# Products of zeros on TensorE in the last four experts of each expert layer

## The reference

```python
def hierarchical_moe(x, w_rg, w_re, w_gate, w_up, w_down):
    """x: (B,S,D). Top-1 expert group, then top-2 SwiGLU experts within it."""
    ...
    for g in range(N_GROUPS):
        hid = jax.nn.silu(jnp.einsum('nd,edf->nef', xt, w_gate[g])) * \
            jnp.einsum('nd,edf->nef', xt, w_up[g])
        hid = hid * combine[:, g, :, None].astype(hid.dtype)
        out = out + jnp.einsum('nef,efd->nd', hid, w_down[g],
                               preferred_element_type=jnp.float32)
    return out.astype(x.dtype).reshape(b, s, d)
```

## Time and profile before

| | us |
|---|---|
| median of 3 runs | 603.98 |
| all runs | 609.18, 601.09, 603.98 |
| the profiled execution | 608.75 |
| its span on the core | 607.0 |
| TensorE (PE) busy | 546.9 (90%) |
| weight loads of TensorE (PEld) busy | 301.7 (50%) |
| VectorE (DVE) busy | 178.7 (29%) |
| ScalarE (ACT) busy | 172.3 (28%) |
| HBM read and written | 388 GB/s over the span |

### The profile page before, as it was taken

The page is one execution under the profiler, slowest core; times in us unless marked ns, Lnnn a source line. Parts: engine busy times, 40 slices in busy tenths (PEclk is TensorE's granted clock), DMA queues, the critical chain, the costliest instruction groups (busy, mean ns, idle before and its releaser), DMA issues.

```text
span 607.0 us, 7989 instructions
## 1 busy us (share of the span) xinstructions
PE 546.9 (90%) x3338; PEld 301.7 (50%) x3338; DVE 178.7 (29%) x306; ACT 172.3 (28%) x307; POOL 6.5 (1%) x16
## 2 busy tenths in 40 slices
PE   5999899999999998668799999999999999987766
PEld 4888687444424441312288878774444344423111
DVE  3686944311101110100374465353111011101001
ACT  4845734111111110000384777341111111100100
POOL 0000000000000000000000000000000000000000
PEclk7999999999999998988799999999999999997877
DMA  8999999899999999999999955598999999999992
GB/s 307 423 420 418 422 419 421 313 425 419 421 421 419 421 421 422 421 419 419 421 419 419 422 211 205 220 423 319 425 421 420 418 421 422 421 419 421 417 419 109
DMA packets 33565, 236.14 MB, mean 389 GB/s; under 512 B 3760, under 2 KB 3760, under 8 KB 5488
## 3 DMA queue, kind: packets, MB, share of 16 engines
q1 hardware_dynamic: 32800, 232.07, 93.0%
q0 software_dynamic: 720, 3.45, 1.4%
HBM read 234.45 MB, written 1.05 MB: 388 GB/s over the span
## 4 chain that ended last, share of the span: by engine, by line
PE 65%; DMA 28%; DVE 3%; ACT 1%; issue 1%; SPq 1%; DVEq 0%; ACTq 0%
PE psum L1263 18%; DMA raw<-stream 18%; DMA late<-stream 9%; PE psum L262 8%; PE psum L263 8%; PE psum L264 8%; PE psum L1240 7%; PE psum L1311 7%; DMA xT<-x_turned 1%; PE psum L519 1%; PE psum L1325 1%; PE psum L336 1%; ACT hid L1384 1%; PE psum L1090 1%; SPq L209 1%
## 5 line engine op out<-in xcount | busy, mean ns | idle before, releaser
L1263 PE MATMUL psum<-raw,x 128*32 128x512 f32 x680 | 91.7, 641 | 22.0 <-DMA raw<-stream 11.8
L254 DVE TENSOR_TENSOR raw_lo<-raw,whi 128x1024 fp32r<-128x1024 f32 x52 | 62.5, 1222 | 47.9 <-ACT whi L247 47.7
L1311 PE MATMUL psum<-y,pickT 128*128 128x512 f32 x128 | 69.5, 668 | 4.5 <-ACT y L1390 3.5
L1240 PEld LDWEIGHTS psum<-pick,h 128*128 128x128 f32 x512 | 59.4, 193 | 18.4 <-issue 15.9
L247 ACT CAST whi<-raw 128x1024 fp32r<-128x1024 f32 x52 | 53.5, 1048 | 48.2 <-PE psum L264 41.3
L1240 PE MATMUL psum<-pick,h 128*128 128x128 f32 x512 | 63.6, 281 | 1.2 <-DVE pick L1207 1.0
L262 PE MATMUL psum<-whi,hnT_hi 128*128 128x512 f32 x144 | 58.1, 403 | 5.4 <-DVE hnT_lo L366 5.2
L1215 DVE TENSOR_TENSOR pick<-pick,lists 128x256 f32<-128x256 f32 x16 | 6.8, 424 | 178.1 <-PE psum L1325 178.1
L263 PE MATMUL psum<-whi,hnT_lo 128*128 128x512 f32 x144 | 57.8, 401 | 0.0
L264 PE MATMUL psum<-raw_lo,hnT_hi 128*128 128x512 f32 x144 | 57.4, 398 | 0.0
L1263 PE MATMUL psum<-raw,hid 128*32 128x512 f32 x376 | 48.8, 619 | 5.9 <-ACT hid L1384 5.1
(11 more groups left out here) (203 smaller groups left out, 493.3 us busy)
## 6 DMA issues: line engine op xcount, KB each, us to landing
raw<-stream SPq DMA_DIRECT2D x157, 1024.0 KB, 26.5
late<-stream SPq DMA_DIRECT2D x60, 1024.0 KB, 24.2
raw<-stream SPq DMA_DIRECT2D x2, 512.0 KB, 7.5
xT<-x_turned SPq DMA_DIRECT2D x2, 512.0 KB, 8.4
h<-x SPq DMA_DIRECT2D x1, 1024.0 KB, 12.3
pb<-even_bias POOLq DMA_DIRECT2D x1, 1024.0 KB, 13.9
pool_c<-even_pool POOLq DMA_DIRECT2D x1, 1024.0 KB, 9.4
pb<-even_bias POOLq DMA_DIRECT2D x1, 512.0 KB, 8.3
```

What stands on the lines that cost most here:

```text
L254: nc.vector.tensor_tensor(raw_lo[PLACE[c][0]][:, cols], chunk(c)[:, cols], whi[:, n % SPLIT, cols].bitcast(F32), ALU.subtract).then_inc(lo ...
L1240: mm = nc.tensor.matmul(psum[:, gather_banks(q)[part], kk * P:(kk + 1) * P], h[:, t, k * P:(k + 1) * P], pick[:, t, :], start=(t == 0), st ...
L1263: nc.tensor.matmul(psum[rows, b, :], lhs[:, rows], chunk(c)[:, e * W4:(e + 1) * W4], start=start, stop=stop).then_inc(moe_used, 1)
L1311: nc.tensor.matmul(bank(b), pickT[:, t * P:(t + 1) * P], y[:], start=(q == 0), stop=(q == QUADS - 1)).then_inc(m.scattered, 1)
```

## The change

`keep_warm_pe` gets a second argument, the PSUM bank that the product writes (3 if none is given). In quad 7 of each layer products of zeros are put between what TensorE does there: three behind each of the chunks k = 1 to 6 (behind the scatter, row scale or turn that follows the chunk, where there is one), five behind the last gate/up chunk, two behind the turn of `hid`, three behind down chunk 1, and three before the last scatter, these into bank 0. In layer 0 five more follow the last scatter. That makes 36 products in layer 0 and 31 in layer 1. No wait and no instruction of another engine changes. From line 280 on the line numbers shift by one, further down by up to twelve.

```diff
--- before.py
+++ after.py
@@ -276,9 +276,10 @@
 
         zeros_ready = sem("zeros_ready")
 
-        def keep_warm_pe(n):
+        def keep_warm_pe(n, b=3):
+
             for _ in range(n):
-                nc.tensor.matmul(bank(3), zeros[:], zeros[:].unsqueeze(1).to_broadcast([P, 4, P]), start=True, stop=True, skip_group_check=True)
+                nc.tensor.matmul(bank(b), zeros[:], zeros[:].unsqueeze(1).to_broadcast([P, 4, P]), start=True, stop=True, skip_group_check=True)
 
 
 
@@ -1341,18 +1342,29 @@
                         row_scale_pe(pe, layer, q)
                     if k == 4 and q:
                         turn_pick_pe(pe, layer, q)
+                    if q == QUADS - 1 and 1 <= k < GU_CHUNKS - 1:
+                        keep_warm_pe(3)
                 if q == 0:
                     turn_pick_pe(pe, layer, q)
                 if q < QUADS - 1:
                     gather_pe(pe, layer, q + 1, (0, 1))
+                if q == QUADS - 1:
+                    keep_warm_pe(5)
                 turn_hid_pe(pe, layer, q)
+                if q == QUADS - 1:
+                    keep_warm_pe(2)
                 for i in range(DOWN_CHUNKS):
                     down_pe(pe, layer, q, i)
+                    if q == QUADS - 1 and i == 1:
+                        keep_warm_pe(3)
                     if i == (1 if q == QUADS - 1 else 2):
                         scatter_pe(pe, layer, q, 0)
                     if q == QUADS - 1 and i == 2 and layer == 0:
                         turn_pe(pe, m.h_added, (2, 4), (0, 1))
+            keep_warm_pe(3, 0)
             scatter_pe(pe, layer, QUADS - 1, 1)
+            if layer == 0:
+                keep_warm_pe(5, 0)
 
         def pickT_act(act, layer, q):
             act.wait_ge(m.pickT_turned, no(layer, q) + 1)
```

## The result

| | before | after |
|---|---|---|
| median, us | 604.16 (6 runs) | 612.18 (6 runs) |
| lowest to highest | 601.09 to 609.18 | 610.88 to 615.25 |
| profiled execution, span | 607.0 | 609.5 |
| TensorE busy | 546.9 | 555.8 |

The ratio is 1.0119, with a 95% interval of 1.0081 to 1.0158. The changed kernel is slower by over 1%, where 601.7 was forecast; 612.18 lies even past the 611.2 that the prediction had as the bound of dear products.

The account below looks back on a forecast made before the run. DMA was taken to bound most of the kernel, TensorE 304 to 499 us and the tail. Layer 0 +1.1 and layer 1 -3.4 sum to -2.3, taken off the median 603.98: 601.7, own range 600 to 603, wide range 597.6 to 606.5.

Parts of the forecast that it names:

- the bound of dear products: Upper bound with 0.42 us for each product, 50 of them on the path: +7.2, giving 611.2 us.
- the step that costs the change in layer 1 by its products alone: Layer 1's last quad: sixth chunk from 581.2, products delay chunks, faster tail ends with last scatter at 598.5, not 601.90: -3.4.
- the sum: Step-by-step addition over both layers' last quads at 0.23 us per further product: +1.1 - 3.4 = -2.3 us.
- Rival C: Larger gain: new code length removes layer 0's 0.85 gap and raises the clock earlier, 599.2; or cheaper products, 597.6; chance 0.15.
- 216 ns product: Alternative price from the skill's figure: 67 products take 14.5 us instead of 15.4, the part on the path 0.5 less.
- Layer 0: Layer 0's last quad: groups delay the eighth chunk by 4.6, the faster tail wins part back; +1.1 us, all reaching the end.
- The step from one execution to the median: Profiled 608.75 becomes 606.45; the same difference taken off the median of three runs, 603.98, gives 601.7.
- Rival A: Layer 0, gate/up chunks 2 to 7: backlog wins, a little slower; at 0.31 per product 605.7; chance 0.25 together with D.
- Rival B: Tails stay at 1.2 GHz and products only cost: layer 0 +3.7, layer 1 +1.2, so 608.9; chance 0.07.
- D: No change at all: what layer 1 gains, layer 0 loses; 604; chance 0.25 together with Rival A.
- the split by 2%: Chances for the whole kernel: faster by over 2% 0.03, no change 0.94, slower 0.03.

Follow-up runs that it names:

- e7: Changed kernel plus 8 products in layer 1's skipped spill code, moving layer 1's restart by 16 instructions; 606.28 us, ratio to the kernel before 1.0031.
- e2: Changed kernel with the products of layer 1 alone; 603.74 us, ratio to the kernel before 1.0004.
- e4: Changed kernel plus 24 products in layer 0's skipped spill code, moving both layers' restarts by 48 instructions; 604.2 us, ratio to the kernel before 1.0003.
- e0: The kernel before once more, without any edit, for a second trace; 604.27 us, ratio 1.001.
- e8: Changed kernel with products in layer 1 alone, without groups behind chunks 1 to 4, plus 24 skipped products in either layer; 604.96 us, ratio to before 1.0.
- e6: Kernel before plus 24 products in the skipped spill code of either layer, so both restarts move; 606.1 us, ratio 1.0022.
- e9: Changed kernel without groups behind chunks 1 to 4 in both layers, plus 24 skipped products in layer 0; 601.23 us, ratio to before 0.9924.
- e1: Kernel before plus 36 products in layer 1's skipped spill code, putting its restart where the changed kernel has it; 604.75 us, ratio 1.001.
- e10: e9 plus 116 skipped products in layer 1, its restart 256 instructions behind its place in the changed kernel; 605.26 us, ratio to before 1.0027.
- e3: Changed kernel with the products of layer 0 alone; 605.99 us, ratio to the kernel before 1.0024.

## Why the prediction was wrong

- **What failed** is the step that costs the change in layer 1 by its products alone, from the old timeline, in which the two chunks behind the restart have no gap (it set out from 581.2). The products of layer 0 also moved layer 1's code, by 72 instructions, and the sum had no term for that. It measured 5.9 (e7 against after). In the timelines, restart to last scatter took 32.95 (571.43 to 604.38) where the sum has 26.6, and -3.4 for the layer came out as +3.0. Rival C had the mechanism, a gap behind the branch that the code's new length may move, but priced it only as a gain in layer 0. In layer 0 it could not move, since every product stands behind it. In layer 1, where it could, C did not look, and its other sign was not in the range.
- **The mechanism of the products was right, the exact total partly luck.** With no edge near, restart to last scatter took 26.7 (e2), 26.8 (e4) and 26.6 (e7), where the sum has 598.5 - 571.92 = 26.6. Two small errors cancelled. From one chunk's start to the next with a group between them e4 took 1.89 (582.05 to 583.94), put at 1.00 + 0.77, and from the third gate/up chunk to the last scatter all three took 20.7, where the sum has 598.5 - 578.15 = 20.35. From the restart to the third chunk they took 5.9 to 6.1, where it has 578.15 - 571.92 = 6.23. The size that failed is this last one in the changed kernel: 12.25. (The 216 ns product would have taken 0.7 us off 50 products on the path, not the 0.5 that stands there; nothing rests on it.)
- **Layer 0** was put at +1.1 and came to -0.3 (L0 40.1 for 40.4): the eighth chunk was late by 2.9 and not 4.6, mostly because the clock came back almost 4 us earlier (at 274.5 and not 278.4). That moment varies from execution to execution. In the second trace of before it was early too.
- **The step from one execution to the median** was the second mistake. I took the same difference off the median, but that execution, near the top of the six timed runs, had both tails at 1.2 GHz; e0 had one and a half of them at 2.4. Of the 10.5 us between forecast and median, 4.8 lie between the two profiled executions (608.75 to 611.24, where -2.3 was forecast) and 5.7 in this step: 608.75 stood 4.8 above the median that the forecast set out from, 611.24 0.9 below its own. In the medians the same products win nothing: e4 equals before (1.0003), with 10 runs within 3.4 us where 31 of before span 8.9. They save where a tail would have run at 1.2 GHz, and cost where it would not: from restart to the second turn of h layer 0 took 32.2 in e4, and without products 34.1 with a tail at 1.2 GHz (e8) and 31.7 with one mostly at 2.4 (e6). One trace each, so the sizes are rough. The saving of one trace must be weighed with how often its state occurs, and the prediction should have had that as a rival. The Trainium skill ("TensorE: Matmul & The Clock Gate", Part 1) says that one kernel shows different numbers of slow matmuls from run to run. It says so of the warm-up at a kernel's start; the two traces of before show it in the tails.
- **Rival A**, the backlog, was right in kind: four groups with no wait to hide in are what e9 leaves out, and e9 is 3.0 faster than e4 by the medians. Its price of 0.28 or more for a product was not reached (20.7 for 20.35 over the 28 products behind the third chunk's start is 0.01 each on top of what the sum had). **Rival B** did not occur: behind the eighth chunk the clock stayed at 1.00 to the last scatter in every layer that had products there. **C** in layer 0 was sized about right: it put the gap of 0.85 and the late clock at 2.5, and L0 is 40.4 in e7, which has the gap, and 38.4 in e4, which has not (medians 606.28 and 604.2, intervals overlapping). **D** has e4's number, 604, but e4 also has the restarts moved. And the split by 2% came out as put at 0.94: no change.
- The pause costs more the more backlog TensorE has: nothing that the medians show without products (e1), 4 to 6 with few (e10 against e9), 5.9 with all. In the timelines of e1 and e3 the DMA waits of the last chunks are what is gone behind the pause; with all products these waits are filled already.

## What to carry to other kernels

Instructions that are added move all code behind them. Where a kernel jumps over long code, look at the records right behind the jump in both kernels: a pause that "issue" ends, while the data has landed, can be a fetch of instructions. Two things tell: a packet of the instruction queue shortly before it ends, and whether it goes when some instructions inside the skipped code move the target. Work put into waits should stay shorter than the wait it sits in, since the slack that it takes is what would absorb a later stall. And before a saving is taken from a trace at a low clock, find out how often that state occurs.

## What the runs showed of the hardware

- TensorE's restart behind the jump over the spill code took 3.9 to 5.8 us, and 2.6 to 2.8 us of that lie behind the start of the recorded instruction packet. A second packet follows 5.6 to 5.9 us after the first, in both layers of all 14 traces, with a pause or not. In the traces with a pause TensorE went on 2.4 to 2.7 us after that packet had started, behind the same 3 records each time. The Trainium skill ("Runtime: NRT & Kernel Launch", "Instruction fetch mechanics") says that a taken branch whose target is not at hand waits for a fetch, and that fetches are in blocks of 16 KiB, which are 256 instructions. This agrees with the packets here (the q8 line of the profile's page has 32 of them with 0.52 MB in the changed kernel) and with e10, where a restart 256 instructions on has the pause behind the same 3 records. That the second block is late as well, and costs 3.6 to 3.9 us where the edge is near, stands in these runs.
- The pause's length hardly varied: 3.63, 3.64, 3.74, 3.83 and 3.94 us in five traces with the same 3 records before it.
- A pause of 3.6 to 3.9 us shortly behind a restart kept the granted clock at 0.50 for long: it was back at 1.00 9.1 to 10.4 us behind the restart (five traces), against 3.0 to 4.0 us without the pause (nine traces).
- In the 14 traces, the clock was at 1.00 through all 17 tails with products behind the last gate/up chunk. Of the 11 tails without them, 8 were wholly or partly at 0.50.
- The granted clock at the same instruction differed between executions of one program: in the two traces of before, layer 0's scatter took 3.65 and 1.95.
